# Lag blocks of layer 0 in another order: two behind the transforms, six in twos and ones behind the first gate products

## The chip, the core and the metric

One core of a Trainium2 chip runs the whole program in one launch. The metric is the time on the device in microseconds. Engines are named TensorE (PE), VectorE (DVE), ScalarE (ACT), and SP, which only issues DMAs. The matrix products are in float32; 128 partitions by 512 columns is a bank of PSUM, and there are eight banks.

## The reference

The program is a block of two layers over 256 latent and 256 context tokens of width 1024. Each layer mixes tokens by a Fourier branch and a state-space branch (S5) on the same normalised input, gates both, projects them, and then mixes channels (dense in layer 0, eight experts in layer 1). What matters here is the token mixer:

```python
def token_mixer(...):
    p_lat = a_lat @ w_in
    p_ctx = a_ctx @ w_in                      # layer 0
    y_ctx, y_lat = s5_branch(s_ctx, p_lat[..., OFF_SSM:OFF_GA], ...)
    out_lat = merge_branches(p_lat, y_lat, w_four, w_glu_a, w_glu_b, w_out)

def merge_branches(p, y_s, w_four, w_glu_a, w_glu_b, w_out):
    g_a = jax.nn.sigmoid(p[..., OFF_GA:OFF_GB])
    g_b = jax.nn.sigmoid(p[..., OFF_GB:])
    y_a = fourier_mix(p[..., :OFF_SSM]) @ w_four
    y_b = (y_s @ w_glu_a) * jax.nn.sigmoid(y_s @ w_glu_b)
    return (g_a * y_a + g_b * y_b) @ w_out
```

`s5_branch` is, per direction, `h = diag_scan(bu, lam_bar, ...)` and `y = d * u + (h @ c_mat).real`.

## The kernel before

All data lie transposed, channels on partitions and the 512 tokens along the columns (`NT`). Each engine has a program of its own, written out by hand in the order in which it is to run; they meet only through semaphores. The order of the code is the order on the engine.

The scan of the state-space branch works in chunks of 8 tokens. Within a chunk the response is a Toeplitz matrix per group of 16 channels, built from **lags**; between chunks a short scan over 64 chunk states `H` runs on VectorE. For layer 0 there are eight sets of parameters, n = 0 to 7 (two directions of four blocks of channels). For each set:

- VectorE makes the output powers, `out_powers(0, n)` (eight instructions, L1199 to L1158), into `CW0` for even n and `CW1` for odd n. For n of 2 and more it first waits until lag block n-2 has been computed (it read that buffer) and until the store of set n-2 has landed.
- ScalarE masks the input matrix, `masked(0, n)`, into `LB0` or `LB1` (L695, two instructions); for n of 2 and more it waits for lag block n-2.
- TensorE computes the lag block, `lags(0, n)`: eight matmuls of 32 by 128 (L1630, recorded as 16) from `CW` and `LB` of the same parity. Blocks 0 to 3 are summed in one bank, 4 to 7 in another.
- ScalarE stores the powers to HBM (`cks`), `store_reads(0, n)` (L721, 512 KB in pieces of 512 bytes). They are read back as the weights `ck` of the Y products.

When four blocks are done, VectorE evacuates the bank (`lag_rows`, L1213 and L1217), ScalarE stores it to `gds` (`store_lags`, L727), and when both halves have landed SP reads them back as Toeplitz matrices (`toep_load`, L576, eight issues into `GR`, the buffer of the transforms). After the second half ScalarE also reloads `raw` with the parameters of layer 1 (L854).

Around this stand, on TensorE and in this order: the two Fourier transforms (`dft1`, 16 products, `dft2`, 8 products), the sums of modulation tile 8 (`mod_sums`, L1591), the eight products of gate b (gb0 to gb7, L1648, 8 matmuls each; gb0 to gb3 read the ring tile `w_in` 4, gb4 to gb7 `w_in` 5), the sums of tile 9 between gb5 and gb6, and then the **Y products** in two halves: 128 small matmuls with the weights `ck` (L1851) and 32 with `toep` (L1859) each. Every product leaves by an evacuation on ScalarE (L767). Then follow `ya` with the turns of layer 1, `glub`, `glua`, `out`, the dense mixer, and layer 1.

Weights come through three ring buffers of 2 MB. SP issues the loads in one fixed order (L559), each when the tile three places earlier has had its last use: modulation tile 9 when gb3 has ended (it takes the place of `w_in` 4), then the first `ck` tile, then `toep`, then the second `ck` tile when gb7 has ended, then `w_four`, then modulation tile 10.

Before the change two lag blocks stand behind each of gb0 to gb3. On ScalarE, behind the evacuation of gb0 to gb3, stand two stores and, up to gb2, two masks; masks 0 and 1 are made long before. The first store of lags stands ahead of the evacuation of gb3, the second behind that of gb4.

Of the kernel before, what the change touches and what calls it, by code (L numbers as in the profile page):

```python
# [27 lines left out]
ACT = mybir.ActivationFunctionType  # L28
# [7 lines left out]
NT = CTX + SEQ  # L36
# [22 lines left out]
FFN_MOD = 12  # L59
ITS = 2 * MB  # L60
HALF_C = NCH // 2


C_ID, C_ONE, C_SEL, C_E16, C_MC = 0, 128, 256, 264, 280
# [41 lines left out]
def program(nc, a, out, bps, cks, gds, uds, yds):  # L106

    top = ExitStack()
    with top:
# [253 lines left out]
        G2 = GR[:, 0:SLOT].rearrange("p (k t) -> p k t", k=KD)  # L363
# [165 lines left out]
        def _(sp):  # L529
# [50 lines left out]
            def ys_move(l, mh):  # L580

                n = NCH - HALF_C * l
                for c in range(2):
# [65 lines left out]
        def _(act):  # L649
# [20 lines left out]
            def mod_rows(t):  # L670

                if t % 4 < 3:
                    return
                act.wait_ge(mod_rows_done, t + 1)
                if t >= 4:
                    act.wait_ge(mod_cols_done, t // 4)
                nc.scalar.activation(mrow[:], ps[:, 2, :], ACT.Copy).then_inc(mod_rows_taken, 1)
# [38 lines left out]
            def store_reads(l, n):  # L716

                b = n % 2
                o = 0 if n % 2 == 0 else SG
                act.wait_ge(c_made, ITS * l + n + 1)  # L720
                act.dma_start(cks[2 * l + n // 4][:, D * (n % 4):D * (n % 4) + D].rearrange("p (a c) -> p a c", a=8),  # L721
                              CWs[b][:].rearrange("p r g c -> p (r g) c")[:, :, o:o + P]).then_inc(cw_stored[b], 16)
# [18 lines left out]
            def stage_y(l, mh):  # L741

                n = NCH - HALF_C * l
                for c in range(2):
# [20 lines left out]
            def evac(key, dst, func=ACT.Copy, cols=NT):  # L765
                bank, free = arrived(act, key)
                nc.scalar.activation(dst, bank[:, 0:cols], func).then_inc(free, 1)  # L767
# [33 lines left out]
            for l in range(DEPTH):  # L801
                t0 = CTX * l
                n = NT - t0
                root("ss", l, 0)
                if l == 0:
                    mod_rows(2)
                    mod_rows(3)
                shift(l, 0)
                for m in range(4):
                    stage_u(l, m)  # L810
                    if l == 0 and m == 1:
                        mod_rows(4)
                if l == 0:
                    for k in range(4):
                        evac(("ga", l, k), G[:, k, t0:NT], ACT.Sigmoid, n)
                        turned(0, 2 * k)
                        turned(0, 2 * k + 1)
                        if k == 1:
                            mod_rows(5)
                    masked(0, 0)  # L820
                    masked(0, 1)
                    for k in range(4, 8):
                        evac(("ga", l, k), G[:, k, t0:NT], ACT.Sigmoid, n)
                        if k == 5:
                            mod_rows(6)
                for m in range(4):
                    evac(("f", l, m), uF[:, m, t0:NT], cols=n)
                    if l == 0 and m == 1:
                        mod_rows(7)
                for m in range(4):  # L830
                    for t in range(2 * l, 4):
                        evac(("dft1", l, m, t), Q[:, t, m, :], cols=2 * P)
                for m in range(4):
                    for s in range(l, 2):
                        evac(("dft2", l, m, s), uF[:, m, s * 256:s * 256 + 256], cols=256)
                if l == 1:
                    for m in range(8):
                        evac(("ga", l, m), G[:, m, t0:NT], ACT.Sigmoid, n)
                if l == 0:
                    mod_rows(8)  # L840
                for m in range(8):
                    if l == 0 and m == 3:
                        store_lags(0, 0)
                    evac(("gb", l, m), G2[:, m, t0:NT], ACT.Sigmoid, n)
                    if l == 0 and m < 4:
                        for i in range(2 * m, 2 * m + 2):
                            store_reads(0, i)
                        for i in range(2 * m + 2, 2 * m + 4):
                            if i < ITS:
                                masked(0, i)  # L850
                    if l == 0 and m == 4:
                        store_lags(0, 1)
                        act.wait_ge(b_masked, 2 * ITS)
                        act.dma_start(raw[:].rearrange("p a r c h -> p (a r c h)"), a["bc"][1]).then_inc(raw_in, 16)  # L854
                    if l == 0 and m == 5:
                        mod_rows(9)
                stage_y(l, 0)
                stage_y(l, 1)
                if l == 0:
                    for m in range(8):  # L860
                        turned(1, m)
                    mod_rows(10)
                for m in range(8):
                    if l == 0 and m >= 4:
                        masked(1, m - 4)
                        store_reads(1, m - 4)
                    evac(("glub", l, m), aT[:, m, t0:NT], ACT.Sigmoid, n)
                if l == 0:
                    mod_rows(11)
                    act.wait_ge(mix_ready, 8)  # L870
                    weights_high(0)
                    for k in range(4, 8):
                        masked(1, k)
                        store_reads(1, k)
                    for mh in range(2):
                        store_lags(1, mh)
                    weights_high(1)
                root("ss", l, 1)
                shift(l, 1)
                if l == 0:  # L880
                    ahead = 2
                    for part, size in enumerate(PARTS):
                        m0 = part * PARTS[0]
                        for m in range(m0, m0 + size):
                            if m - m0 >= 2:
                                taken(act, ("up", l, m - 2))
                            evac(("gate", l, m), sg[:, m % 2, :], ACT.Silu)
                            if m > m0:
                                hidden_high(m - 1, m0)
                            if m % 2:  # L890
                                if m == m0 + size - 1:
                                    hidden_high(m, m0)
                                weights_high(ahead)
                                if 3 <= ahead < ADA_TILES - FFN_MOD + 3:
                                    mod_rows(FFN_MOD + ahead - 3)
                                ahead += 1
                        for t in range(4):
                            if ahead < len(split_tiles) - 1:
                                weights_high(ahead)
                            if 3 <= ahead < ADA_TILES - FFN_MOD + 3:  # L900
                                mod_rows(FFN_MOD + ahead - 3)
                            ahead += 1
# [673 lines left out]
        def _(pe):  # L1576
# [155 lines left out]
            for l in range(DEPTH):  # L1732
                t0 = CTX * l
# [72 lines left out]
                for m in range(4):  # L1806
                    for s in range(l, 2):
# [5 lines left out]
                                      (Q[:, t, m, P:2 * P], con[:, C_SN + 256 * k:C_SN + 256 * k + 256])]  # L1813
                        product(("dft2", l, m, s), pairs, 256)
                if l == 0:
                    mod_sums(8)
                if l:
                    pe.wait_ge(a_copied, KD)
                for name, tile in ((("gb", 4),) if l == 0 else (("ga", 2), ("gb", 4))):
                    for h in range(2):  # L1820
                        w = slot(("w_in", l, tile + h))[:].rearrange("p (k c) -> p k c", k=KD)
                        for m in range(4):
                            product((name, l, 4 * h + m),
                                    [(w[:, k, P * m:P * m + P], aT2[:, k, :] if l else aT[:, k, :]) for k in range(KD)], n_)
                            if l == 0 and h == 0:
                                if m == 0:
                                    mod_turn(8)
                                lags(0, 2 * m)
                                lags(0, 2 * m + 1)
                            if l == 0 and (h, m) == (1, 1):  # L1830
                                mod_sums(9)
                        if l == 0 and h == 1:
                            mod_turn(9)
                n = NCH - HALF_C * l
                for mh in range(2):
# [4 lines left out]
                    for i in range(8):  # L1840
                        m, g = 2 * mh + i // 4, i % 4
# [13 lines left out]
                    for i in range(8):  # L1855
                        m, g = 2 * mh + i // 4, i % 4
# [225 lines left out]
            for j in range(4):  # L2082
                for i_ in range(2):
                    m = 2 * j + i_
# [95 lines left out]
```

## Time and profile before

| what | us |
|---|---|
| median of 3 runs | 2105.9 |
| lowest, highest | 2104.84, 2110.22 |
| the profiled execution | 2107.13 |
| its span, first to last instruction | 2105.3 |
| TensorE busy | 2036.1 (97%) |
| VectorE busy | 1388.0 (66%) |
| ScalarE busy | 930.3 (44%) |

The mean granted clock of TensorE is 0.98 of full speed. The gate products of layer 0 run from 199 to 272 us. In the rows further down, L numbers are lines of the kernel before; a row of the timeline merges like instructions that follow each other, and the bracket at its end gives the idle time of the engine ahead of it and what ended that. A matmul in float32 is recorded as two instructions, so that a product of eight appears as x16.

### The profile page before, as it was taken

To read this page: it belongs to the slowest core of one execution; us is meant where nothing else is said; L and a number is where in the kernel's file an instruction comes from. 1 tells how busy PE (TensorE), PEld (TensorE's weight loads), DVE (VectorE), ACT (ScalarE), POOL (GpSimd) and SP (SyncE) were. 2 spreads that over 40 slices of the span, in tenths; PEclk is the share of its full clock that TensorE was granted. 3 is DMA by queue.
4 is the path that set the end of the run, shared out by engine and by line. 5 is a ranking of instruction groups with operands and counts; after the bars stand their busy time and mean duration, and the time that the engine had idled before them with its cause. 6 is when DMAs were issued, how large, how long until landed. Compare 5 with 4: busy or idle time off the path is not lost.

```text
span 2105.3 us, 24542 instructions
## 1 busy us (share of the span) xinstructions
PE 2036.1 (97%) x10074; PEld 1538.5 (73%) x10074; DVE 1388.0 (66%) x1863; ACT 930.3 (44%) x849; POOL 0.2 (0%) x4
## 2 busy tenths in 40 slices
PE   5999899999999999999989999999999999999998
PEld 2456364447777777788977888888888888888886
DVE  6674635662232333646248898898989888898987
ACT  2212112121221221311117777677776776677675
POOL 0000000000000000000000000000000000000000
PEclk9999999989999999999989999999999999999999
DMA  9342695333435441268538999899998999999994
GB/s 399 87 159 100 187 254 185 125 110 116 165 140 220 160 168 59 113 200 200 180 120 302 377 351 373 336 362 374 358 366 332 374 365 359 362 336 375 357 369 182
DMA packets 83840, 529.27 MB, mean 251 GB/s; under 512 B 23057, under 2 KB 49553, under 8 KB 52753
## 3 DMA queue, kind: packets, MB, share of 16 engines
q1 hardware_dynamic: 62976, 508.65, 65.8%
q10 hardware_dynamic: 20752, 19.05, 2.7%
q8 instruction: 81, 1.33, 0.2%
q14 instruction: 31, 0.25, 0.0%
HBM read 509.39 MB, written 18.28 MB: 251 GB/s over the span
## 4 chain that ended last, share of the span: by engine, by line
PE 92%; DVE 4%; DMA 2%; ACT 1%; issue 1%; SPq 0%; DVEq 0%; ACTq 0%
PE ps L1648 20%; PE ps L2044 14%; PE ps L2029 14%; PE ps L2030 14%; PE ps L1657 6%; PE ps L1661 6%; PE ps L1664 6%; PE ps L1591 2%; PE ps L1851 1%; PE ps L1975 1%; DMA ring<-in_w_mod 1%; PE ps L1791 1%; PE ps L1859 1%; PE ps L1958 1%; DVE WL L1473 1%; PE ps L1615 1%
## 5 line engine op out<-in xcount | busy, mean ns | idle before, releaser
L1473 DVE TENSOR_TENSOR WL<-mring,WH 128x2048 fp32r<-128x2048 f32 x336 | 755.2, 2287 | 107.8 <-ACT WH L919 107.7
L919 ACT ACTIVATE WH<-mring 128x2048 fp32r<-128x2048 f32 x336 | 626.1, 1913 | 142.5 <-PE ps L2044 97.8
L2029 PE MATMUL ps<-WH,XGh 128*128 128x512 f32 x896 | 355.5, 397 | 2.4 <-ACT WH L919 2.4
L2030 PE MATMUL ps<-WH,XGl 128*128 128x512 f32 x896 | 351.0, 392 | 0.0
L2044 PE MATMUL ps<-WL,XGh 128*128 128x512 f32 x896 | 221.6, 389 | 0.0
L1281 DVE TENSOR_TENSOR ringl<-ring,FWH 128x4096 fp32r<-128x4096 f32 (+2 forms) x21 | 82.2, 3917 | 185.9 <-ACT FWH L778 185.9
L1648 PE MATMUL ps<-aT,ring 128*128 128x512 f32 (+1 forms) x576 | 200.1, 507 | 0.0
L2029 PEld LDWEIGHTS ps<-WH,XGh 128*128 128x128 f32 x896 | 169.3, 189 | 36.7 <-issue 2.5
L2030 PEld LDWEIGHTS ps<-WH,XGl 128*128 128x128 f32 x896 | 169.3, 189 | 34.0
L2044 PEld LDWEIGHTS ps<-WL,XGh 128*128 128x128 f32 x896 | 168.2, 188 | 34.9
L778 ACT ACTIVATE FWH<-ring 128x4096 fp32r<-128x4096 f32 (+2 forms) x21 | 67.9, 3232 | 283.4 <-DMA ring<-in_ffn_gu 166.2
L2029 PE MATMUL ps<-WH,hTh 128*128 128x512 f32 x448 | 175.9, 393 | 0.0
L2030 PE MATMUL ps<-WH,hTl 128*128 128x512 f32 x448 | 174.6, 390 | 0.0
L1648 PEld LDWEIGHTS ps<-aT,ring 128*128 128x128 f32 x576 | 110.0, 193 | 85.4 <-issue 78.7
L2044 PE MATMUL ps<-WL,hTh 128*128 128x512 f32 x448 | 110.7, 389 | 0.0
L2029 PEld LDWEIGHTS ps<-WH,hTh 128*128 128x128 f32 x448 | 84.2, 188 | 17.1
L2030 PEld LDWEIGHTS ps<-WH,hTl 128*128 128x128 f32 x448 | 84.2, 188 | 17.0
L2044 PEld LDWEIGHTS ps<-WL,hTh 128*128 128x128 f32 x448 | 83.9, 188 | 17.3
L1657 PE MATMUL ps<-aTh,FWH 128*128 128x512 f32 x352 | 93.7, 405 | 2.0 <-ACT aTh L792 2.0
L1661 PE MATMUL ps<-aTl,FWH 128*128 128x512 f32 x352 | 93.0, 403 | 0.0
L1664 PE MATMUL ps<-aTh,ringl 128*128 128x512 f32 x352 | 90.7, 401 | 0.0
L1657 PEld LDWEIGHTS ps<-aTh,FWH 128*128 128x128 f32 x352 | 66.8, 192 | 26.8 <-issue 9.0
(275 smaller groups left out, 2210.6 us busy)
## 6 DMA issues: line engine op xcount, KB each, us to landing
mring<-in_moe_gate SPq DMA_DIRECT2D x56, 2048.0 KB, 9.7
mring<-in_moe_up SPq DMA_DIRECT2D x56, 2048.0 KB, 9.7
mring<-in_moe_down SPq DMA_DIRECT2D x56, 2048.0 KB, 9.6
ring<-in_w_mod SPq DMA_DIRECT2D x23, 2048.0 KB, 8.0
ring<-in_w_in SPq DMA_DIRECT2D x11, 2048.0 KB, 10.2
ring<-in_ffn_gu SPq DMA_DIRECT2D x11, 2048.0 KB, 10.9
cks<-CW ACTq DMA_DIRECT2D x16, 512.0 KB, 3.1
ring<-cks SPq DMA_DIRECT2D x4, 2048.0 KB, 12.2
```

The lines of the kernel that those rows point to most:

```text
L778: nc.scalar.activation(FWH[i % 2][:, 0:w_], ring[n_ % RING][:, 0:w_], ACT.Copy).then_inc(w_high, 1)
L919: nc.scalar.activation(WH[buf][:, o], mring[t % MRING][:, o], ACT.Copy).then_inc(high_done, 1)
L1281: V.tensor_tensor(ringl[s_][:, 0:w_], ring[s_][:, 0:w_], FWH[i % 2][:, 0:w_].bitcast(F32), ALU.subtract).then_inc(w_low, 1)
L1473: V.tensor_tensor(WL[buf][:, o], mring[t % MRING][:, o], WH[buf][:, o].bitcast(F32), ALU.subtract).then_inc(low_done, 1)
L1591: last = mm(ps[g:g + 8, 2, :], silu4[:, k, t % 4, :], wv[:, k, :], start=(t % 4 == 0 and k < 4), stop=(t % 4 == 3 and k >= 4), skip_group_ ...
L1648: last = mm(bank[:, 0:cols], w, x, start=(k == 0), stop=(k == len(pairs) - 1))
L1657: mm(bank, wh[:, k, :], xh[:, k, :], start=(k == 0), stop=False)
L1661: mm(bank, wh[:, k, :], xl[:, k, :], start=False, stop=False)
L1664: last = mm(bank, wl[:, k, :], xh[:, k, :], start=False, stop=(k == n - 1))
L2029: mm(out_, ah, WH[buf][:, o:o + 512], start=(first and q == 0), stop=False)
L2030: mm(out_, al, WH[buf][:, o:o + 512], start=False, stop=False)
L2044: last = mm(out_, ah, WL[buf][:, o:o + 512], start=False, stop=(final and q == len(pairs) - 1))
```

## The change

The eight lag blocks of layer 0 are spread otherwise. Blocks 0 and 1 stand behind the second transform, ahead of the sums of modulation tile 8. Behind gb0 stand blocks 2 and 3, behind gb1 block 4, behind gb2 blocks 5 and 6, behind gb3 block 7. ScalarE follows in the same order: stores 0 and 1 stand between the evacuations of the first and the second transform, masks 2 and 3 behind those of the second; behind each of gb0 to gb3 stand the stores of that product's blocks, and then the masks two further on. The two stores of the lags stand together behind gb3, with the reload of `raw`. VectorE's and SP's programs are as they were. No instruction is added or taken away.

```diff
+LAG_AT = ((2, 3), (4,), (5, 6), (7,))
...
                 for m in range(4):
                     for t in range(2 * l, 4):
                         evac(("dft1", l, m, t), Q[:, t, m, :], cols=2 * P)
+                if l == 0:
+                    for i in range(2):
+                        store_reads(0, i)
                 for m in range(4):
                     for s in range(l, 2):
                         evac(("dft2", l, m, s), uF[:, m, s * 256:s * 256 + 256], cols=256)
...
                 if l == 0:
+                    for i in range(2):
+                        masked(0, i + 2)
                     mod_rows(8)
                 for m in range(8):
+                    evac(("gb", l, m), G2[:, m, t0:NT], ACT.Sigmoid, n)
+                    if l == 0 and m < 4:
+                        for i in LAG_AT[m]:
+                            store_reads(0, i)
+                        for i in LAG_AT[m]:
+                            if i + 2 < ITS:
+                                masked(0, i + 2)
                     if l == 0 and m == 3:
                         store_lags(0, 0)
-                    evac(("gb", l, m), G2[:, m, t0:NT], ACT.Sigmoid, n)
-                    if l == 0 and m < 4:
-                        for i in range(2 * m, 2 * m + 2):
-                            store_reads(0, i)
-                        for i in range(2 * m + 2, 2 * m + 4):
-                            if i < ITS:
-                                masked(0, i)
-                    if l == 0 and m == 4:
                         store_lags(0, 1)
                         act.wait_ge(b_masked, 2 * ITS)
...
                 if l == 0:
+                    lags(0, 0)
+                    lags(0, 1)
                     mod_sums(8)
...
                                 if m == 0:
                                     mod_turn(8)
-                                lags(0, 2 * m)
-                                lags(0, 2 * m + 1)
+                                for n in LAG_AT[m]:
+                                    lags(0, n)
```

What this gives on the engines follows; L numbers of the changed kernel are its own, from one to seven higher. First TensorE, from the second transform (`con,GR`) on: L1630 or L1635 is a lag block, L1591 or L1596 the modulation sums, L1648 or L1653 with `aT,ring1` a gate product. Before:

```order
L1648 MATMUL ps<-con,GR 128x256 x32
L1591 MATMUL ps<-ring2,silu4 8x512 x8
L1648 MATMUL ps<-aT,ring1 128x512 x8
L1630 MATMUL ps<-CW0,LB0 32x128 x8
L1630 MATMUL ps<-CW1,LB1 32x128 x8
L1648 MATMUL ps<-aT,ring1 128x512 x8
L1630 MATMUL ps<-CW0,LB0 32x128 x8
L1630 MATMUL ps<-CW1,LB1 32x128 x8
L1648 MATMUL ps<-aT,ring1 128x512 x8
L1630 MATMUL ps<-CW0,LB0 32x128 x8
L1630 MATMUL ps<-CW1,LB1 32x128 x8
L1648 MATMUL ps<-aT,ring1 128x512 x8
```

and after:

```order
L1653 MATMUL ps<-con,GR 128x256 x32
L1635 MATMUL ps<-CW0,LB0 32x128 x8
L1635 MATMUL ps<-CW1,LB1 32x128 x8
L1596 MATMUL ps<-ring2,silu4 8x512 x8
L1653 MATMUL ps<-aT,ring1 128x512 x8
L1635 MATMUL ps<-CW0,LB0 32x128 x8
L1635 MATMUL ps<-CW1,LB1 32x128 x8
L1653 MATMUL ps<-aT,ring1 128x512 x8
L1635 MATMUL ps<-CW0,LB0 32x128 x8
L1653 MATMUL ps<-aT,ring1 128x512 x8
L1635 MATMUL ps<-CW1,LB1 32x128 x8
L1635 MATMUL ps<-CW0,LB0 32x128 x8
```

Blocks 0 and 1 have moved ahead of the sums and of gb0, and one block fewer stands behind gb1.

ScalarE, from the evacuations of the first transform (`GR<-ps 128x256`) to those of gb0 (`GR<-ps 128x512`); `uF` is the second transform's, L721 or L722 a store of powers, L695 or L696 a mask. Before:

```order
L767 ACTIVATE GR<-ps 128x256 x16
L767 ACTIVATE uF<-ps 128x256 x8
L767 ACTIVATE GR<-ps 128x512
L721 DMA cks<-CW0 128x8x128
L721 DMA cks<-CW1 128x8x128
L695 ACTIVATE LB0<-raw,con 128x2x4x16 x2
L695 ACTIVATE LB1<-raw,con 128x2x4x16 x2
```

and after:

```order
L768 ACTIVATE GR<-ps 128x256 x16
L722 DMA cks<-CW0 128x8x128
L722 DMA cks<-CW1 128x8x128
L768 ACTIVATE uF<-ps 128x256 x8
L696 ACTIVATE LB0<-raw,con 128x2x4x16 x2
L696 ACTIVATE LB1<-raw,con 128x2x4x16 x2
L768 ACTIVATE GR<-ps 128x512
```

The first two stores have moved ahead of the evacuations of the second transform, and the masks of sets 2 and 3 ahead of gb0.

ScalarE again, from the store behind gb2 to the reload of `raw` (L854 or L859); L727 or L728 is a store of the lags. Before:

```order
L721 DMA cks<-CW0 128x8x128
L721 DMA cks<-CW1 128x8x128
L695 ACTIVATE LB0<-raw,con 128x2x4x16 x2
L695 ACTIVATE LB1<-raw,con 128x2x4x16 x2
L727 DMA gds<-Gs0 128x2x240
L767 ACTIVATE GR<-ps 128x512
L721 DMA cks<-CW0 128x8x128
L721 DMA cks<-CW1 128x8x128
L767 ACTIVATE GR<-ps 128x512
L727 DMA gds<-Gs1 128x2x240
L854 DMA raw<-in_bc 128x2048
```

and after:

```order
L722 DMA cks<-CW1 128x8x128
L722 DMA cks<-CW0 128x8x128
L696 ACTIVATE LB1<-raw,con 128x2x4x16 x2
L768 ACTIVATE GR<-ps 128x512
L722 DMA cks<-CW1 128x8x128
L728 DMA gds<-Gs0 128x2x240
L728 DMA gds<-Gs1 128x2x240
L859 DMA raw<-in_bc 128x2048
L768 ACTIVATE GR<-ps 128x512 x4
```

The store of set 6 now stands behind gb2 and only that of set 7 behind gb3, where both stores of the lags and the reload follow at once; before, the second of them stood behind gb4.

## Rows read from the trace of the kernel before

**Rows 1.** Timeline of TensorE, 195 to 295 us: start, length, what, and [idle before]
```profile
197.31 1.90 PE L1591 MATMUL ps<-ring,silu 128*8 128x512 f32 x16
199.14 7.13 PE L1648 MATMUL ps<-aT,ring 128*128 128x512 f32 x16
206.21 1.08 PE L1630 MATMUL ps<-CW,LB 128*32 128x128 f32 x32
...
218.15 1.08 PE L1630 MATMUL ps<-CW,LB 128*32 128x128 f32 x16 [3.22 <-DVE CW L1158]
219.16 9.60 PE L1648 MATMUL ps<-aT,ring 128*128 128x512 f32 x16
...
229.71 7.13 PE L1648 MATMUL ps<-aT,ring 128*128 128x512 f32 x16
...
240.30 0.64 PE L1630 MATMUL ps<-CW,LB 128*32 128x128 f32 x16 [2.88 <-DVE CW L1158]
240.87 15.70 PE L1648 MATMUL ps<-aT,ring 128*128 128x512 f32 x32
...
258.33 14.00 PE L1648 MATMUL ps<-aT,ring 128*128 128x512 f32 x32
...
279.60 3.79 PE L1859 MATMUL ps<-pack,GR 128*128 128x64 f32 x32
283.31 7.41 PE L1851 MATMUL ps<-H,ring 64*128 64x64 f32 x128
```

**Rows 2.** TensorE by stretch: length, busy (count), granted clock, DMA share, GB/s
```profile
218.00:225.00 7.00, 6.85 (x24) 0.56 0.25 75
104.00:112.00 8.00, 6.90 (x168) 1.00 0.78 291
455.00:460.00 5.00, 1.88 (x29) 0.97 0.84 351
460.00:475.00 15.00, 14.43 (x23) 0.50 0.02 9
```

**Rows 3.** Timeline of VectorE, 178 to 233 us, same columns
```profile
185.86 0.69 DVE L1158 SCALAR_TENSOR_TENSOR CW<-rms,CW 128x512 f32<-128x512 f32 x1
209.99 0.20 DVE L1199 COPY CW<-raw 128x64 f32<-128x64 f32 x1 [23.45 <-DMA cks<-CW]
...
214.06 0.20 DVE L1199 COPY CW<-raw 128x64 f32<-128x64 f32 x1
...
232.15 0.20 DVE L1199 COPY CW<-raw 128x64 f32<-128x64 f32 x1 [4.82 <-DMA cks<-CW]
```

**Rows 4.** Timeline of ScalarE, 150 to 275 us; ACTq is its DMA issue
```profile
177.12 6.86 ACT L767 ACTIVATE GR<-ps 128x256 f32<-128x256 f32 x16 [0.73 <-PE ps L1648]
...
249.75 0.37 ACTq L727 DMA_DIRECT2D gds<-Gs  x1
```

**Rows 5.** Timeline of SP's DMA issues, 236 to 273 us
```profile
237.32 0.35 SPq L559 DMA_DIRECT2D ring<-cks  x1
255.17 10.88 SPq L576 DMA_DIRECT2D GR<-gds  x8
272.42 0.34 SPq L559 DMA_DIRECT2D ring<-cks  x1
```

**Rows 6.** DMA issues at 237.3, 249.75, L576, at 263 and 272.4: count, KB, us to landing
```profile
ring<-cks SPq DMA_DIRECT2D x1, 2048.0 KB, 14.4
cks<-CW ACTq DMA_DIRECT2D x1, 512.0 KB, 16.1
...
gds<-Gs ACTq DMA_DIRECT2D x1, 240.0 KB, 5.4
...
L576 SPq DMA_DIRECT2D GR<-gds x8: 325/1200/2947, 255.2 to 263.1; - x8
...
GR<-gds SPq DMA_DIRECT2D x1, 256.0 KB, 14.0
...
ring<-cks SPq DMA_DIRECT2D x1, 2048.0 KB, 9.8
```

## The prediction

> **What bounds the kernel now.** I first read the chain of work that ended last, around 200 us. It is TensorE nearly all the way, but at two places it leaves TensorE: it goes to a DMA that writes `CW` to `cks`, then to VectorE, which makes the next two sets of output powers, and only then back. The timeline of TensorE shows the same as two idle gaps ahead of lag blocks, 3.22 us at 218.15 and 2.88 us at 240.30 [rows 1]. The reader is to see the loop behind each. `CW` and `LB` have two buffers. The store of set n is issued by ScalarE only behind the evacuation of a gate product, and VectorE may not write set n+2 before that store has landed. The product gb0 ends at about 206.25 and VectorE, idle for 23.45 us, starts set 2 at 209.99 [rows 3]: a turnaround of 3.74 us. A set takes 4.07 us (209.99 to 214.06), so two take 8.1, more than the 7.1 us of one gate product that stands between the lag blocks.
>
> The second thing to see is the clock. After the first gap the granted clock averages 0.56 over 218 to 225 [rows 2], the lower of its levels (1.2 against 2.4 GHz) for most of it. The lag block there takes 1.08 against 0.64 at 240.30, gb2 takes 9.60 against 7.13 for gb0; and gb4 with gb5, behind the second gap, take 15.70 against 14.00 for gb6 with gb7 [rows 1].
>
> **The change part by part.** All times are on the trace's own clock. No arithmetic is added: eight lag blocks, eight stores and sixteen masks remain.
>
> *Lags 0 and 1 ahead of gb0.* They cost 1.04 us there (the 32 matmuls at 206.21 end where gb1 starts) and 1.04 less behind gb0, so nothing net; they start at 197.31 where the modulation sum starts now [rows 1]. Their powers were ready at 186.55 [rows 3], their masks long before. The two stores go ahead of the evacuations of the second transform. ScalarE is through with the first transform at 183.98 [rows 4] and waits for set 1 until 186.55, some 2.6 us. The results of the second transform can wait that long: its eight products end at 197.31 [rows 1] and start at about 183.4, so they come 1.7 apart, and with four banks TensorE wants the first bank back only 7 us after the start. I cost it at nothing; without those banks it would be up to 2 us. The stores land long before 197.
>
> *Powers 2 and 3 under gb0.* VectorE waits only for the lag blocks, starts at about 197.9 and is done at 206.0. gb0 ends at 207.25 (199.14, plus 1.04, plus 7.07). Lags 2 and 3 no longer wait: the gap of 3.22 goes, and with it the low clock behind it, 0.44 on the lag block and 2.47 on gb2. What is late next? Stores 2 and 3 leave at 207.25, powers 4 start 3.74 later at 211.0 and end at 215.05, just ahead of the end of gb1 (208.3 + 7.07 = 215.35). Here only lag 4 stands. Powers 5 end at 219.1, the rows of the first half take 1.06 (232.15 less 4.82 is 227.33; four sets from 209.99 end at 226.27) [rows 3], powers 6 run from 220.2 to 224.25. gb2 ends at 223.0, lag 5 at 223.6, and lag 6 waits **0.7 us**. gb3 ends at 224.9 + 7.07 = 231.95. Store 5 left at 223.0, so powers 7 run from 226.75 to 230.8 and lag 7 does not wait: the gap of 2.88 goes, and the 1.70 of low clock on gb4 and gb5.
>
> *Sum for TensorE.* gb4 starts at 232.55, where it is 240.87 now [rows 1]: 8.3 us, which is 3.22 + 2.88 + 0.44 + 2.47 less 0.7. With the 1.70 TensorE stands at the end of the gate products **10.0 us** earlier. A gap of 0.7 should not lower the clock: in 104 to 112 TensorE has a gap of 1.1 and the clock stays at 1.00 [rows 2].
>
> *What the gain then meets.* The Y products need two transfers. `toep` writes the lag matrices into the transform buffer, and it waits for the store of the second half of the lags; the reads `ck` of the second half are a 2 MB ring load behind it on SP's queue. Now the eight `toep` issues start at 255.17 [rows 5], the last starts at 263.1 and lands 14.0 later, at 277.1 [rows 6], and TensorE first reads them at 279.60: 2.5 us to spare. The second `ck` load is issued at 272.42 and lands 9.8 later [rows 5, 6], at 282.2, where TensorE reads it at 283.31 [rows 1]: **1.1 us** to spare. It lands 5.1 behind `toep`, and alone a load of its size would not need 9.8: it stands behind `toep` in one queue. So I must ask when `toep` starts after the change. Its start hangs on the end of gb3, because the loads of the ninth modulation tile and of the first `ck` wait for that. They leave at the end of gb3 (236.84; 237.32 for the `ck` load [rows 5]), and that load takes 14.4 us, to 251.7 [rows 6]. Meanwhile ScalarE's small transfers starve: a store to `cks` takes 16.1 us there [rows 6], against less than 3.74 at 206. The lag store issued at 249.75 [rows 4] lands 5.4 later [rows 6], 3.4 behind the end of that `ck` load.
>
> After the change gb3 ends 4.9 us earlier, not 10.0; the second half of the 10.0 is won behind it. ScalarE now issues the second lag store at about 234, right into the starving, instead of at 249.75, so its earlier place in the code gains nothing by itself. It does stand behind less: store 6 left at 224.3 and is out of the way. The `ck` load lands at 232.4 + 14.4 = 246.8, and of store 7 and two lag stores I take 2.2 us instead of 3.4 for the rest, since one 512 KB store of the two has gone (bounds: 1.0, if the stores had trickled through, and 3.4, as now). `toep` starts at 249.0, lands 21.9 later at 270.9, and is wanted at 269.6 (279.60 less 10.0): a new wait of 1.3. Its products take 3.71 (283.31 less 279.60), to 274.6; the second `ck` load lands 5.1 behind `toep`, at 276.0: another 1.4. The Y products of the second half thus start at 276.0, not 283.31: **7.3 us** earlier. The bounds give 6.1 and 8.5.
>
> Two facts of queues are weighed here. The row shows that beside the two ring loads a 512 KB store takes 16.1 us [rows 6]. The Trainium skill, "DMA: Bandwidth & Descriptors", section on queues, rings and completion order, says that each DMA engine takes turns between its queues packet by packet, and that within one ring descriptors are consumed in order. If turns gave ScalarE's queue an even share, its lag store would land soon after 234 and no wait would be left (the first rival). The trace agrees with turns only in so far as the store crawls rather than stops, and with the order inside a ring, by which the `ck` load stands behind `toep`. That order speaks against this change.
>
> Behind the Y products everything up to the end is released by TensorE's own progress (ya with its turns in step with VectorE, glub, the loads), so I carry the 7.3 us to the end. The profiled execution took 2107.13 (span 2105.3), 1.2 above the median of 2105.9. It would be 2099.8, the median **2098.6**.
>
> **The rivals.**
> *First, no wait in the Y products*: the lag store gets through beside the ring loads and `toep` starts before 246.3 (255.17 less 8.9, since the tighter of the two margins takes up 1.1 of the 10.0). For it: `toep`'s data is ready at 234. Against it: 16.1 us for one store. Gain 10.0: 2095.9.
> *Second, the new waits lower the clock.* 1.3 and 1.4 us lie 3.7 us apart. For it: 3.1 us idle within 455 to 460 were followed by 0.50 over 460 to 475 [rows 2]. Against it: the gap in 104 to 112 cost nothing. A short stretch, as on gb4 and gb5, costs 1.7: gain 5.6, 2100.3.
> *Third, the gaps stay in the gate products*: powers 6 wait for a store that is a microsecond later than I have it, the 0.7 becomes 1.7 and the clock falls as at 218. That costs 1.0 + 0.4 + 2.5 and moves gb3 and all that hangs on it: gain 3.4, 2102.5. The change would do half of what it says.
> *Fourth, slower*: one mechanism, the clock in the Y products. If the waits for `toep` and `ck` set off a fall as long as that of 460 to 475, 15 us and more at half rate [rows 2], it takes back 7.5 us, more than the 6.1 that is left at the late bound of `toep` (start at 250.2): 1.4 slower, 2107.3. It decides from the point where the two waits together pass the 3.1 us idle of 455 to 460, i.e. when `toep` starts after 249.4. Against it: TensorE is busy for 3.7 us between them.
>
> **How the numbers follow.** Forecast as summed, 2098.6 with about 1.3 either way: 0.47. First rival 0.22, second 0.18, third 0.08, fourth 0.05. A measurement can tell about 0.3% of this kernel from no change, 6.3 us, so faster means below 2099.6. That holds for the first rival and three quarters of the forecast: 0.22 + 0.35 = 0.57. The same: the rest of the forecast, the second and third rivals, most of the fourth, 0.40. Slower by over 0.3%: 0.03, the fourth with a longer fall than any in the trace. The range goes from 2094.5 (all of the 10.0, the 0.7 of lag 6 too, and a little of the spread of the runs before) to 2103.5 (the third rival and a microsecond), leaving out about one tenth above and less below.
>
> **What the new profile would show.** The gaps ahead of lag blocks 3 and 7 gone, one of 0.7 ahead of lag 6; clock at 1.00 from 200 to 262; gb4 starting near 232.5; `toep` issued near 249; a gap of 1 to 2 us ahead of the first product that reads it and one ahead of the second `ck` group, both put down to DMA. The forecast is wrong if `toep` starts well before 247 or after 251, if the clock falls behind a small gap, or if anything past 300 is not moved by the same amount as the Y products.

## The result, and the profile after

The changed kernel is slower: median 2115.6 us against 2105.9 (six runs of each), ratio 1.0038 with a 95% interval of 1.0025 to 1.005. 2098.6 was forecast. The profiled execution took 2108.97 (span 2107.1) and is the fastest of its six; a second profile, of the same kernel in another job, took 2117.19 (span 2115.4). The two show the same things in different sizes, so both are read here.

First the timeline of TensorE of the changed kernel, as in [rows 1]: start, length, engine, line, what, and in brackets the idle time ahead and what ended it. L1635 is a lag block, L1653 with `aT,ring` a gate product, L1858 the small Y matmuls with `ck`, L1866 those with `toep`.

```profile
195.91 1.08 PE L1635 MATMUL ps<-CW,LB 128*32 128x128 f32 x32
...
214.80 0.65 PE L1635 MATMUL ps<-CW,LB 128*32 128x128 f32 x16 [0.95 <-DVE CW L1163]
...
223.91 0.64 PE L1635 MATMUL ps<-CW,LB 128*32 128x128 f32 x16 [0.83 <-DVE CW L1163]
...
232.13 14.00 PE L1653 MATMUL ps<-aT,ring 128*128 128x512 f32 x32
...
261.82 7.40 PE L1858 MATMUL ps<-H,ring 64*128 64x64 f32 x128
270.04 4.61 PE L1866 MATMUL ps<-pack,GR 128*128 128x64 f32 x32 [0.82 <-DMA GR<-gds]
275.41 13.92 PE L1858 MATMUL ps<-H,ring 64*128 64x64 f32 x128 [0.76 <-DMA ring<-cks]
289.26 7.09 PE L1866 MATMUL ps<-pack,GR 128*128 128x64 f32 x32
296.13 4.34 PE L1653 MATMUL ps<-uF,ring 128*128 128x512 f32 x5
```

The gate products came out nearly as the sum had them: the gaps of 3.22 and 2.88 are gone, gaps of 0.95 and 0.83 have come, and gb4 with gb5 take 14.00. Then the Y products: two waits for DMAs, 0.82 for `toep` and 0.76 for the `ck` load, both of them forecast. But behind the first of them the first `toep` group takes 4.61 where it took 3.79 [rows 1], the `ck` matmuls of the second half (64, recorded as 128) 13.92 where they took 7.41 at 283.31 [rows 1], and the last group 7.09. The same stretch in TensorE's clock (columns: stretch, length, busy, granted clock, DMA share, GB/s), first of the changed kernel,

```profile
220.00:245.00 25.00, 24.17 (x100) 1.00 0.64 227
...
274.00:284.00 10.00, 9.24 (x84) 0.50 1.00 406
284.00:296.00 12.00, 12.00 (x82) 0.50 0.27 74
296.00:310.00 14.00, 13.64 (x41) 0.85 0.68 199
```

and of the kernel before:

```profile
220.00:245.00 25.00, 22.12 (x102) 0.85 0.49 169
...
274.00:284.00 10.00, 10.00 (x146) 1.00 1.02 385
284.00:296.00 12.00, 12.00 (x157) 1.00 0.77 251
```

The low stretch has moved: from the gate products, where the clock was 0.85 over 220 to 245, to the Y products. Shorter stretches show where it begins:

```profile
270.00:272.50 2.50, 2.46 (x22) 1.00 0.97 406
272.50:273.00 0.50, 0.50 (x6) 0.80 1.15 492
273.00:274.65 1.65, 1.65 (x8) 0.50 1.00 427
```

The clock falls between 272.5 and 273, some 2.8 us behind the wait of 0.82, which ended at 270.04, and before the wait of 0.76, which lies from 274.65 to 275.41. So the first wait alone preceded the fall. The clock is back in the first ya product, at about 300: some 27 us at half rate. SP's issues in the changed kernel show that the transfers went as reckoned:

```profile
232.10 0.35 SPq L560 DMA_DIRECT2D ring<-cks  x1
248.64 10.57 SPq L577 DMA_DIRECT2D GR<-gds  x8
261.98 0.34 SPq L560 DMA_DIRECT2D ring<-cks  x1
```

`toep` was issued at 248.64, against 255.17 before [rows 5]; 249.0 was forecast. The next row is the second `ck` load.

In the second profile of the changed kernel (label e1 below) the wait for `toep` is longer, and nothing of the Y products behind it runs at full clock:

```profile
197.15 1.08 PE L1635 MATMUL ps<-CW,LB 128*32 128x128 f32 x32
...
262.35 7.40 PE L1858 MATMUL ps<-H,ring 64*128 64x64 f32 x128
272.11 7.09 PE L1866 MATMUL ps<-pack,GR 128*128 128x64 f32 x32 [2.36 <-DMA GR<-gds]
279.12 13.92 PE L1858 MATMUL ps<-H,ring 64*128 64x64 f32 x128
...
299.85 5.02 PE L1653 MATMUL ps<-uF,ring 128*128 128x512 f32 x8
```

Executions start with loads of slightly different length, so times are best compared from a common point: the end of the second transform (197.31 in the kernel before [rows 1], 195.91 and 197.15 in these two).

| from the end of the second transform to | before | changed | changed, second profile |
|---|---|---|---|
| first Y matmul | 74.9 | 65.9 | 65.2 |
| first ya product | 97.0 | 100.2 | 102.7 |
| modulation sums of tile 10 | 135.6 | 140.8 | 142.7 |

So 9.0 to 9.7 us are gained before the Y products, and 12.3 and 15.5 given back in them: 22.0 us of Y products take 34.3 and 37.5. Another 2.0 and 1.4 are lost by the sums of tile 10, since ya starts at half clock. Together the stretch is 5.2 and 7.1 us longer.

### The profile page after: what moved, and what is told of

The parts are those of the page before. It is cut to its first block, busy times and chain, and to the rows that moved or that the text cites. A ratio compares the mean times of both kernels' runs of the same rounds, so it can differ in the third digit from the quotient of the medians.

```text
span 2107.1 us, 24542 instructions
## 1 busy us (share of the span) xinstructions
PE 2038.8 (97%) x10074; PEld 1543.3 (73%) x10074; DVE 1388.3 (66%) x1863; ACT 930.2 (44%) x849; POOL 0.2 (0%) x4
## 4 chain that ended last, share of the span: by engine, by line
PE 92%; DVE 4%; DMA 3%; ACT 1%; issue 1%; SPq 0%; DVEq 0%; ACTq 0%
PE ps L1653 20%; PE ps L2051 14%; PE ps L2036 14%; PE ps L2037 14%; PE ps L1662 6%; PE ps L1666 6%; PE ps L1669 6%; PE ps L1596 2%; PE ps L1858 1%; DMA GR<-in_w_mod 1%; PE ps L1982 1%; PE ps L1796 1%; PE ps L1866 1%; DVE WL L1478 1%; PE ps L1965 1%; PE ps L1620 1%
## 5 line engine op out<-in xcount | busy, mean ns | idle before, releaser
L1653 PE MATMUL ps<-aT,ring 128*128 128x512 f32 (+1 forms) x576 | 195.9, 500 | 0.0
L1653 PEld LDWEIGHTS ps<-aT,ring 128*128 128x128 f32 x576 | 108.7, 190 | 82.3 <-issue 75.8
```

The lines of the kernel that those rows point to most:

```text
L1653: last = mm(bank[:, 0:cols], w, x, start=(k == 0), stop=(k == len(pairs) - 1))
```

## The experiments

In the rows of each kernel the L numbers are its own, a few lines apart; the Y products are told by `H,ring` (with `ck`) and `pack,GR` (with `toep`), the first ya product by `uF,ring`. Ratios are to the kernel before, run in the same job.

**e1, the changed kernel again.** No edit.

> The changed kernel once more, for a second profile beside the first, since the profiled execution (2109.0) was the fastest of its six and the median was 2115.6. Theory A (two short waits of TensorE for DMAs in the Y products set off a fall of the clock, and the Y products, made of small matmuls, do not bring it back): median 2113 to 2117; a stretch at about 0.50 begins in the Y products of layer 0, near 274, and reaches past 300; where the time is near 2115, it reaches into the ya products. Theory B (the clock is by chance, and something behind 340 us costs the time): the low stretch is absent or elsewhere, and the time is lost behind 340.

Median 2113.1, ratio 1.0033 (1.0022 to 1.0044). The low stretch begins in the Y products, as theory A has it, and reaches past 300. It ends about 302.5, within the first ya product. Of the 10.1 us by which this span is longer than that of the kernel before, 7.1 are lost ahead of tile 10's sums and 3 behind 340, so theory B does not explain the time.

```profile
284.00:296.00 12.00, 12.00 (x100) 0.50 0.56 161
296.00:310.00 14.00, 13.65 (x48) 0.76 0.38 97
```

**e2, `toep` read back in two halves.** This takes away what makes TensorE wait.

```diff
-            def toep_load(l):
-                sp.wait_ge(g_stored, 16 * 2 * (l + 1))
+            def toep_load(l, mh):
+                sp.wait_ge(g_stored[mh], 16 * (l + 1))
...
-        stream += mods(6) + [("w_in", 0, 0)] + mods(7) + [("w_in", 0, 4)] + mods(8) + [("w_in", 0, 5)] + mods(9)
-        stream += [("ck", 0, 0), ("toep", 0, 0), ("ck", 0, 1), ("w_four", 0, 0)] + mods(10)
+        stream += mods(6) + [("w_in", 0, 0)] + mods(7) + [("w_in", 0, 4)] + mods(8) + [("w_in", 0, 5), ("toep", 0, 0)] + mods(9)
+        stream += [("ck", 0, 0), ("toep", 0, 1), ("ck", 0, 1), ("w_four", 0, 0)] + mods(10)
...
+                    if l == 0 and m == 2:
+                        store_lags(0, 0)
                     if l == 0 and m == 3:
-                        store_lags(0, 0)
                         store_lags(0, 1)
...
-                    if mh == 0:
-                        pe.wait_ge(toep_in, 16 * CHUNK * (l + 1))
+                    pe.wait_ge(toep_ins[mh], 16 * CHUNK * (l + 1))
```

> The changed kernel with the Toeplitz matrices of layer 0 and 1 read back in two halves: the first half as soon as its store has landed, ahead of modulation tile 9 on SP's queue, the second in the old place. Its lag store stands behind gb2. The wait for toep and for the second ck load should both go. Theory A: no gap in the Y products, clock 1.00 through them, TensorE at the first ya product 10 us earlier than in the kernel before, time 2095 to 2098. Theory B: the waits (1.6) go and no more, time about 2113.

Median 2098.2, ratio 0.9962 (0.9948 to 0.9976), faster than the kernel before. No wait stands in the Y products any more, and their lengths are those of the full clock:

```profile
196.62 1.08 PE L1641 MATMUL ps<-CW,LB 128*32 128x128 f32 x32
...
215.77 0.65 PE L1641 MATMUL ps<-CW,LB 128*32 128x128 f32 x16 [1.22 <-DVE CW L1167]
...
262.79 7.40 PE L1864 MATMUL ps<-H,ring 64*128 64x64 f32 x128
270.12 3.79 PE L1871 MATMUL ps<-pack,GR 128*128 128x64 f32 x32
273.84 7.41 PE L1864 MATMUL ps<-H,ring 64*128 64x64 f32 x128
281.18 3.79 PE L1871 MATMUL ps<-pack,GR 128*128 128x64 f32 x32
284.80 3.65 PE L1659 MATMUL ps<-uF,ring 128*128 128x512 f32 x8
```

From the end of the transform to ya it is 88.2 us, 8.8 less than before, where 10 was forecast. This is what the new order is worth when no wait follows from it. Yet e2 differs from the changed kernel in its transfers too, so the next experiment keeps the transfers of the changed kernel and fills the waits, and e4 puts a wait into the kernel before.

**e3, the waits filled with work.** All transfers as in the changed kernel.

```diff
+                    if l == 0 and mh == 1:
+                        mm(bank_for(pe, ("ya", 0, 0)), ident, aT[:, 2, :], start=True, stop=True)
...
+                    if l == 0 and mh == 0:
+                        for q in range(2):
+                            mm(bank_for(pe, ("ya", 0, 0)), ident, aT[:, q, :], start=True, stop=True)
                     if mh == 0:
                         pe.wait_ge(toep_in, 16 * CHUNK * (l + 1))
```

> The changed kernel with three additional matmuls of 512 columns on data at rest (into the bank that the first ya product overwrites): two ahead of the first product that reads toep, one ahead of the second half of the Y products. They take 2.6 us and lie where TensorE otherwise waits 1.6 us; all transfers stay as they are. Theory A: hardly any idle time is left there, the clock stays at 1.00, time 2097 to 2101. Rival C (the late transfers cost the time, whatever TensorE does meanwhile, and the clock falls by the small matmuls alone): time as the changed kernel or up to 2.6 more, 2115 to 2118, clock low there.

Median 2099.8, ratio 0.9975 (0.9962 to 0.9988). Three matmuls more, and 13 us less than the changed kernel in the same job:

```profile
197.21 1.08 PE L1635 MATMUL ps<-CW,LB 128*32 128x128 f32 x32
...
270.61 1.98 PE L1864 MATMUL ps<-aT,con 128*128 128x512 f32 x4
272.43 3.68 PE L1871 MATMUL ps<-pack,GR 128*128 128x64 f32 x32
275.95 1.08 PE L1844 MATMUL ps<-aT,con 128*128 128x512 f32 x2
276.95 7.41 PE L1860 MATMUL ps<-H,ring 64*128 64x64 f32 x128
...
287.92 3.65 PE L1653 MATMUL ps<-uF,ring 128*128 128x512 f32 x8
```

`toep` was issued at 249.79, 52.6 behind the end of the second transform, as in both profiles of the changed kernel (52.7), so the transfers were no earlier; TensorE only was not idle for them. Rival C falls. What was put in is dense work, so e3 does not tell whether small matmuls in the waits would have done as well. Two of its nine times are 2105.7 and 2105.9, with a mean granted clock of 0.981 against 0.983 to 0.987 in the other seven; where their clock was low was not seen.

**e4, one short wait put into the kernel before.** The order of the lag blocks is the old one.

```diff
+                if key == ("ck", 0, 1):
+                    sp.dma_start(brt[:], a["brt"]).then_inc(delayed, 16)
+                    sp.wait_ge(delayed, 16)
                 src = tile_src(key)
```

> The kernel before, with the second ck load of layer 0 issued about 2 to 5 us later (behind a 4 KB load that must land first). TensorE then waits 1.5 to 4 us ahead of the second half of the Y products, and nothing else is changed. Theory A: the clock falls behind this wait, and the time is 10 to 16 longer than before, 2114 to 2122. Rival C: only the wait itself is added, 2107.5 to 2110.

Median 2116.0, ratio 1.0035 (1.0015 to 1.0055). The second `ck` load left 3.9 us later, but the wait is shorter than I expected, 0.70 us, since most of the delay went into spare time. It does the same harm:

```profile
282.73 12.64 PE L1855 MATMUL ps<-H,ring 64*128 64x64 f32 x128 [0.70 <-DMA ring<-cks]
295.30 7.09 PE L1863 MATMUL ps<-pack,GR 128*128 128x64 f32 x32
302.18 4.89 PE L1652 MATMUL ps<-uF,ring 128*128 128x512 f32 x8
```

Its ten times lie in two groups: three from 2103.3 to 2105.2, as the kernel before, and seven from 2115.5 to 2120.2. Their mean granted clocks part in the same way, 0.981 to 0.984 in the three and 0.976 to 0.978 in the seven (0.977 in the profile). In the profile the fall costs some 10 us besides the wait: 8.5 in the small matmuls and 1.2 in the first ya product. Only one execution has a profile, so it is not shown whether the three fast ones had the wait and no fall, or no wait.

**e5, dense work behind the fall.**

```diff
+                    if l == 0 and mh == 1:
+                        for q in range(8):
+                            mm(bank_for(pe, ("ya", 0, 0)), ident, aT[:, q, :], start=True, stop=True)
                     banks = [bank_for(pe, ("Y", l, mh, c)) for c in range(2)]
```

> The changed kernel with eight additional matmuls of 512 columns on data at rest between the two halves of the Y products, behind the wait for the second ck load, so that both waits stay. They take 7 us at full clock, 14 at half. Theory A (once low, the clock stays low as long as only the small Y matmuls run; dense matmuls bring it back): low from about 272, back at 1.00 by the end of the added matmuls, the second half of the Y products in 11 us instead of 21, and the time no more than 4 above or below the changed kernel although 7 us of work are added, 2108 to 2117. Rival D (the fall has a fixed length, or the added work brings nothing back): the second half still takes 18 to 21, time 2120 to 2130.

Median 2111.0, ratio 1.0023 (1.0012 to 1.0034). The first wait (1.70) was followed by the fall, the second shrank to 0.23, the eight added matmuls (L1846) took 9.07, and the second half of the Y products behind them ran at full clock:

```profile
273.24 4.99 PE L1869 MATMUL ps<-pack,GR 128*128 128x64 f32 x32 [1.70 <-DMA GR<-gds]
278.47 9.07 PE L1846 MATMUL ps<-aT,con 128*128 128x512 f32 x16 [0.23 <-DMA ring<-cks]
287.47 7.40 PE L1861 MATMUL ps<-H,ring 64*128 64x64 f32 x128
294.79 3.79 PE L1869 MATMUL ps<-pack,GR 128*128 128x64 f32 x32
298.41 3.65 PE L1653 MATMUL ps<-uF,ring 128*128 128x512 f32 x8
```

```profile
274.00:278.00 4.00, 4.00 (x28) 0.70 0.95 406
278.00:284.00 6.00, 5.76 (x11) 0.63 1.02 431
284.00:290.00 6.00, 6.00 (x53) 1.00 0.76 240
```

Work of 9 us was added and the time is 2.2 below that of the changed kernel in e1 (another job, so this difference itself is not firm). What is firm is the pair of lengths: 7.40 and 3.79 here, 13.92 and 7.09 in both profiles of the changed kernel. Rival D falls: the low stretch has no fixed length. It lasted some 7 us here, up to the dense work, against 27 in the first profile of the changed kernel.

**e6, the split in the kernel before.**

The edit of e2, with the order of lags and stores as it was.

> The kernel before with toep read back in halves and nothing else. Theory A: there was no wait in the Y products to remove, so the time is that of before within 1 us, 2104 to 2107. Rival (the split itself is what made the earlier run fast): 2099 or less.

Median 2105.5, ratio 1.0001 (0.999 to 1.0013). The split is worth nothing where there is no wait. The gain of e2 is that of the new order, kept.

**e7, stores ahead of the evacuations.** On top of e2:

```diff
-LAG_AT = ((2, 3), (4,), (5, 6), (7,))
+LAG_AT = ((2, 3), (4, 5), (6,), (7,))
...
+                    if l == 0 and m < 3:
+                        for i in LAG_AT[m]:
+                            store_reads(0, i)
+                    if l == 0 and m == 2:
+                        store_lags(0, 0)
                     evac(("gb", l, m), G2[:, m, t0:NT], ACT.Sigmoid, n)
                     if l == 0 and m < 4:
-                        for i in LAG_AT[m]:
-                            store_reads(0, i)
...
                     if l == 0 and m == 3:
-                        store_lags(0, 0)
+                        store_reads(0, 7)
                         store_lags(0, 1)
```

> The changed kernel with toep in halves, and in addition the stores of sets 2 to 6 issued ahead of the evacuation of the gate product behind which their lag blocks stand, and lag blocks (2,3), (4,5), (6), (7) behind gb0 to gb3. Theory A: VectorE no longer waits for stores to land, the two waits of TensorE ahead of lag blocks 4 and 6 (1.2 and 0.8 us) go, the rest is as with the split alone, 1.5 to 2.5 us less than that: 2096. If ScalarE, blocked until a set of powers is made, delays an evacuation that TensorE needs, a new wait ahead of gb2 shows up, and the time is 2098 or more.

Median 2097.4, ratio 0.9954 (0.9937 to 0.997), the lowest of all medians, though it cannot be told from e2 by these times (another job, intervals that overlap); 2096 was forecast. VectorE waits for no store any more. In the profile TensorE's gaps at the lag blocks shrink from 1.22 and 0.83 in e2 to one of 0.20, ahead of lag block 5:

```profile
196.40 1.08 PE L1643 MATMUL ps<-CW,LB 128*32 128x128 f32 x32
...
215.10 0.64 PE L1643 MATMUL ps<-CW,LB 128*32 128x128 f32 x16 [0.20 <-DVE CW L1169]
...
282.66 3.65 PE L1661 MATMUL ps<-uF,ring 128*128 128x512 f32 x8
```

It reaches ya 86.3 us behind the transform, 1.9 less than e2. This, e2 and e3 beat both kernels.

## Why the prediction was wrong

**What bounds the kernel**: right. The loop from store to VectorE to lag block was the cause of both gaps; e7, which takes ScalarE's evacuation out of the loop, removes what was left of them.

**The gate products**: right within a microsecond. From the end of the transform to gb4 it was 43.6 (240.87 less 197.31), 35.2 was forecast, and it is 36.2 and 35.5 (232.65 less 197.15). One term was too small: a turnaround of 3.74 from the end of a gate product to the next set of powers. Behind gb0 the first store of the pair lands 3.2 us after its issue in the kernel before, and 4.8 in the changed one, where VectorE starts set 4 at 210.71, 4.95 behind the end of gb0; so lag 4 waits 0.95. In the second profile it lands after 4.1, and lag 4 waits 0.24. Why the same pair of stores takes longer was not tried.

```profile
205.82 4.78 DMA cks<-CW
...
210.71 0.20 DVE CW L1204
```

That the 0.7 ahead of lag 6 would not lower the clock was right: 0.83 stands there and 0.95 ahead of lag 4, the gate product behind each takes 7.13, and the clock is 1.00 over 220 to 245.

**What the gain meets**: right. Two waits were forecast, for `toep` and for the second `ck` load, 1.3 and 1.4 us. They were 0.82 and 0.76 in one profile, 2.36 and none in the other, and `toep` started at 248.6 and 249.8 against the forecast 249.0. The second `ck` load lands 5.3 behind `toep` in the first profile (13.4 behind its issue at 261.98, so at 275.4, against 270.04), where 5.1 was forecast. The first rival, in which ScalarE's store gets through beside the ring loads, did not come. The chain of the second profile shows the store go out early and starve (start, length, what):

```profile
233.97 15.82 DMA gds<-Gs
258.22 13.85 DMA GR<-gds
```

The store of the second half of the lags, 240 KB, takes 15.8 us and lands at 249.79, where the first `toep` load is issued; the last one, issued at 258.22, ends TensorE's wait at 272.1. In the first profile the same store takes 15.2 us. That ScalarE waits up to 3 us ahead of the evacuations of the second transform cost TensorE nothing, as assumed.

**The step that failed** is the price and the chance of a fall of the clock in the Y products. The fourth rival named the mechanism, two waits that set off a long fall, and gave it 0.05, since it asked for 3.1 us of idle time as at 455 to 460. The second gave a short fall 0.18 and priced it at 1.7, from gb4 and gb5. That price was read from dense work: behind the gaps in the gate products the next matmuls were large, and the clock was back 4 to 6 us behind the end of the gap. In the Y products a wait of 0.70 (e4) or 0.82 was followed by a fall, and the clock stayed low through all that was left of them, 21.0 us of matmuls for the second half where 11.2 were due. The bound of the fourth rival, both waits together past 3.1 us, was none: the two were 1.58, and the clock fell behind the first. The price was 10.7 us in the first profile (12.3 lost less 1.58 waited) and 13.1 in the second (15.5 less 2.36). The 0.83 and 0.95 in the gate products cost no more than themselves in the same execution. So the waits were sized well enough; what differed was where they stood, and I had carried a price from one kind of work to another. My evidence against a fall, the gap of 1.1 in 104 to 112 [rows 2], was sound in itself: it stands ahead of other small matmuls (L1791) and lowered the clock in none of the nine profiles here, nor did gaps of 0.7 to 1.5 in their midst. But those come twice as thick (256 records in 7.9 us of work, against 128 in 7.3 for the `ck` groups), last 8 us and not 22, and have dense products before and behind. Which of these three decides was not tested.

The Trainium skill, "TensorE: Matmul & The Clock Gate", section "Part 1: The HAM clock gate", says that the throttled state is the default and that activity releases it. The runs agree for the dense work of e5, in whose eight matmuls the clock came back. For small matmuls they do not bear it out: in the changed kernel the 80 of a whole half (160 records), with TensorE busy over 284 to 296, ran at 0.50 to their end. Nor does dense work always bring the clock back as soon as in e5: over 460 to 475 it was 0.50 although matmuls of 512 columns kept TensorE busy for 14.43 us [rows 2].

**From the Y products to the end**: only roughly carried. In the first profile 5.2 are lost by tile 10's sums; this execution ended its second transform 1.4 earlier than the kernel before, and it won 1.9 more between the dense mixer of layer 0, at 460, and 1085, part of it since a stretch of low clock in 800 to 870 (0.98 before, 1.00 here) did not occur. That leaves about the 1.8 by which the spans differ. The profiled execution was thus a lucky one, and its time alone understates the loss. In the second profile 7.1 of 10.1 are lost in the stretch.

**What stays open.** By the medians the changed kernel is 9.7 us slower in the first job and 7.7 in the second; two profiles explain 5.2 and 7.1 of it by the Y and ya products. The mean granted clock was 0.974 to 0.978 in the five slower runs of the first job, against 0.981 in the profiled one, so the rest goes with more time at the low clock; where it lies in a typical run was not settled. Why some executions of e4 escape the fall was not tried either.

## What to carry to other kernels

Before removing stalls, list the stretches downstream that are made of small matmuls, and look at the spare time of every transfer that they wait for: if the gain is larger than the spare time, the stall is moved into a place where it may cost much more than its length. Price a short wait by the work around it, not only by its length: here 0.8 us between dense products cost 0.8, and 0.7 to 0.8 in the midst of 22 us of small matmuls cost 10 us and more. Two remedies were cheap here: issue the late transfer in parts as soon as each is ready (e2), or, where that can't be, keep TensorE busy through the wait with dense matmuls (e3).

## What had not been expected of the hardware

- One wait of 0.70 us in the middle of 22 us of matmuls of 64 columns was followed by a fall of TensorE from 2.4 to 1.2 GHz (the profile of e4; by time and mean clock probably in seven of its ten executions), and so was one of 0.82 (changed kernel). Gaps of 0.83 to 1.22 between the gate products, of 512 columns, were not (changed kernel, e2).
- The same small matmuls of the Y products run at full clock from start to end if they enter and are kept at it (22 us), and stay at half if it has fallen (7.40 against 13.92 for 128 records).
- Two stores of 512 KB issued back to back behind gb0 by one engine: the first lands 3.2 us after its issue in the kernel before and 4.1 to 5.1 in the changed kernel and e2.
- A store of 240 KB issued beside two ring loads of 2 MB took 15.2 and 15.8 us to land (changed kernel), against 4.3 and 5.4 in the kernel before, where the one was issued ahead of such loads and the other near their end.
